# An MoE decoder layer on one core: narrower expert visits with two-sum matmuls, and expert rows added up per token in DRAM by GpSimd

## The reference, cut to what matters

```python
top_logit, top_e = lax.top_k(logits, TOP_K)          # 4 of 32 experts for a token
gates = jax.nn.softmax(top_logit, axis=-1)
xs = xf[tok]                                         # rows sorted by expert
hu = lax.ragged_dot(xs, w_gate_up, group_sizes) + b_gate_up[e_sorted]
gate = jnp.minimum(hu[:, :D_FF], SWIGLU_LIMIT)
up = jnp.clip(hu[:, D_FF:], -SWIGLU_LIMIT, SWIGLU_LIMIT)
act = (up + 1.0) * gate * jax.nn.sigmoid(SWIGLU_ALPHA * gate)
y = lax.ragged_dot(act, w_down, group_sizes) + b_down[e_sorted]
out = jnp.zeros_like(xf).at[tok].add(y * g_sorted[:, None])
h = layer_norm(ALPHA_RES * h + out, ln2_g, ln2_b)    # ALPHA_RES = 2 ** 0.25
```

## Time and profile before

| what | value |
|---|---|
| median of 3 runs | 4533.25 us |
| lowest, highest run | 4527.98, 4533.9 us |
| profiled execution, span from first to last instruction | 4529.3 us |
| PE busy | 4289.9 us, 95% of the span |
| DVE, ACT, POOL busy | 3076.1, 1817.6, 1010.1 us |
| DMA | 665.72 MB in all, mean 147 GB/s |

### The profile page before, as it was taken

The page is one execution under the profiler, slowest core; times in us unless marked ns, Lnnn a source line. Parts: engine busy times, 40 slices in busy tenths (PEclk is TensorE's granted clock), DMA queues, the critical chain, the costliest instruction groups (busy, mean ns, idle before and its releaser), DMA issues. The chain is left out here.

```text
span 4529.3 us, 70549 instructions
## 1 busy us (share of the span) xinstructions
PE 4289.9 (95%) x24356; PEld 3153.5 (70%) x24356; DVE 3076.1 (68%) x4861; ACT 1817.6 (40%) x2677; POOL 1010.1 (22%) x1152
## 2 busy tenths in 40 slices
PE   8999988999999998699999999999999999999987
PEld 4444434444444454599989889899999999999961
DVE  2587867878888873555556556666676777777768
ACT  1222223443434433233434444444445555555530
POOL 1111101221111122211112212222222222222235
PEclk9999989999999999799999999999999999999986
DMA  6443330120110010544555456474657667667668
GB/s 194 126 122 92 87 101 16 30 27 21 18 23 16 14 27 19 148 158 148 174 168 190 155 183 220 162 250 161 237 197 239 208 230 241 219 234 237 212 214 362
DMA packets 534140, 665.72 MB, mean 147 GB/s; under 512 B 64416, under 2 KB 402592, under 8 KB 533952
## 3 DMA queue, kind: packets, MB, share of 16 engines
q1 hardware_dynamic: 419664, 501.02, 34.7%
q10 hardware_dynamic: 87744, 77.15, 5.4%
q0 software_dynamic: 26576, 85.56, 5.0%
HBM read 543.61 MB, written 120.03 MB: 147 GB/s over the span
## 5 line engine op out<-in xcount | busy, mean ns | idle before, releaser
L2000 PE MATMUL gu<-x_hi,w_hi 128*128 128x240 f32 (+8 forms) x4096 | 1196.5, 292 | 4.1 <-issue 4.1
L2003 PE MATMUL gu<-x_lo,w_hi 128*128 128x240 f32 (+8 forms) x4096 | 1195.5, 292 | 0.5 <-issue 0.5
L2004 PE MATMUL gu<-x_hi,w_lo 128*128 128x240 f32 (+8 forms) x4096 | 1194.1, 292 | 0.0
L2106 DVE TENSOR_TENSOR w_lo<-w_raw,w_hi 128x2048 fp32r<-128x2048 f32 x386 | 874.6, 2287 | 414.1 <-ACT w_hi L2190 386.2
L2190 ACT ACTIVATE w_hi<-w_raw 128x2048 fp32r<-128x2048 f32 x386 | 726.8, 1908 | 207.4 <-PE gu L2004 132.0
L2000 PEld LDWEIGHTS gu<-x_hi,w_hi 128*128 128x128 f32 x4096 | 774.7, 189 | 4.5 <-issue 4.3
L2003 PEld LDWEIGHTS gu<-x_lo,w_hi 128*128 128x128 f32 x4096 | 773.3, 189 | 1.1 <-issue 0.9
L2004 PEld LDWEIGHTS gu<-x_hi,w_lo 128*128 128x128 f32 x4096 | 773.8, 189 | 0.0
L1972 POOL TENSOR_TENSOR a_lo<-up,a_hi 128x384 fp32r<-128x384 f32 x256 | 396.6, 1549 | 1177.8 <-ACT a_hi L2202 1177.8
L570 PE MATMUL proj_acc<-w_in_sb,hT 128*128 128x512 f32 (+1 forms) x1280 | 499.0, 537 | 0.7 <-ACT hT L586 0.7
L2000 PE MATMUL yp<-w_hi,a_hi 128*128 128x512 f32 x1088 | 445.6, 410 | 2.3
(11 more groups left out here) (316 smaller groups left out, 5878.6 us busy)
## 6 DMA issues: line engine op xcount, KB each, us to landing
w_raw<-w_gate_up SPq DMA_DIRECT2D x258, 1024.0 KB, 7.6
w_raw<-w_down SPq DMA_DIRECT2D x128, 1024.0 KB, 8.1
y_dram<-y_rows ACTq DMA_DIRECT2D x128, 256.0 KB, 2.6
y_dram<-zeros ACTq DMA_DIRECT2D x12, 2688.0 KB, 15.5
h_blk<-h_dram SPq DMA_DIRECT2D x32, 512.0 KB, 8.7
qi_dram<-qi_stage ACTq DMA_DIRECT2D x16, 640.0 KB, 3.2
x_in<-x SPq DMA_DIRECT2D x16, 512.0 KB, 6.1
w_in_sb<-w_in SPq DMA_DIRECT2D x4, 2048.0 KB, 14.2
```

Source lines behind the costliest of these rows:

```text
L2000: op = nc.tensor.matmul(out, s_hi_, m_hi, start=(n == 0), stop=False)
L2003: nc.tensor.matmul(out, s_hi_, m_lo, start=False, stop=False)
L2004: op = nc.tensor.matmul(out, s_lo_, m_hi, start=False, stop=(n == len(pairs) - 1))
L2106: nc.vector.tensor_tensor(w_lo[:, c % 2, cols], raw[:, c % 3, cols], w_hi[:, c % 2, cols].bitcast(F32), ALU.subtract).then_inc(s_lo, 1)
```

## The change

- Widths: `WIDTHS` becomes 384, 352, 320, 304, 288, 272, 256, 240, 208, 176. The counts then give 1, 3, 1, 4, 2, 6, 3, 5, 5 and 2 visits.
- For visits of at most 256 columns (15 of them), `two_sums` replaces `passes` in `up`: w_hi meets x_hi and x_lo in one matmul of 2 x width columns into two halves of a bank, and w_lo meets x_hi in a second one. DVE and ACT get a second body for these (`parted`): ACT copies the second half of both sums out of PSUM (`second_sums`), and DVE adds it to the first half. They work on 256 columns instead of 384.
- `y_dram` and the gathers of `combine_stage` go. `hold_places` and `hold_gates` on POOL make DRAM addresses and gates per row. ACT's `store` multiplies by the gate, and `scatter` on POOL adds each tile's rows into `sums` in DRAM with indirect DMAs (seven per visit). `sums` is first set to h1 in `attend_stage` (a second 512 KB store per block); `combine_stage` only loads it, adds the bias and normalizes, with one DVE pass less. The gates are scaled by 1 / ALPHA_RES.
- POOL's order in a visit: scatter 5 of the visit before; a_lo[0], a_lo[1]; `hold_places`; a_lo[2]; `hold_gates` and the list load of the next visit; a_lo[3]; gather 0; a_lo[4]; gather 1; a_lo[5]; gather 2; a_lo[6]; a_lo[7]; scatters 0 to 4.
- SP: `load_third` (three small value look-ups, a wait on `s_hold`, five small loads) stands before chunk 5 of each visit, and before the first chunk of all. The y stores go from SP and ACT.
- `lists` holds pairs (token, gate). The clearing of `y_dram` in `project_stage` goes (12 DMAs of 2.7 MB); `lists`, `h1` and `sums` get tail rows that are set in `attend_stage`.

```diff
-WIDTHS = tuple(range(ROWS, 2 * P - 17, -GRAIN))
+WIDTHS = (384, 352, 320, 304, 288, 272, 256, 240, 208, 176)
+KINDS = tuple((ROWS - width) // GRAIN for width in WIDTHS)
+LAST_KIND = tuple(kind - 1 for kind in KINDS[1:]) + KINDS[-1:]
+ONE_SUM = sum(width > 2 * P for width in WIDTHS)
...
+                for name in ("h1", "sums"):
+                    sp.dma_start(D_[name][SEQ:, :].rearrange("(m p) n -> p m n", p=P),
+                                 res[:].unsqueeze(1).broadcast_to([P, 1 + ROWS // P, D])).then_inc(s_clear, 16)
...
+                def load_third(v):
+                    at = look_up(sp, v, 1, MOST)
                     rest, few = (look_up(sp, v, what, 1) for what in (2, 3))
-                    rows, cols = [], []
+                    if not first(v):
+                        sp.wait_ge(s_hold, v)
                     for i in range(4):
...
+                        row = at + 2 * P + i * FEW - rest * ((i - i % 2) * FEW) - few * (i % 2 * FEW)
+                        sp.dma_start(third[i * FEW:(i + 1) * FEW], D_["lists"][bass.ds(row, FEW), :]
+                                     ).then_inc(s_third, 16)
...
+                    sp.dma_start(spot[:], A["spots"][bass.ds(rest + few, 1)].rearrange("o p j n -> (o p) j n")
+                                 ).then_inc(s_third, 16)
...
+                        if c == 5:
+                            load_third(v + 1)
...
+                def list_rows(v):
+                    at = look_up(pool, v, 1, MOST)
                     if not first(v):
                         pool.wait_ge(s_x, 48 * v)
                         pool.wait_ge(s_xt, 8 * v)
                     nc.gpsimd.dma_start(who[:], D_["lists"][bass.ds(at, ROWS), :].rearrange(
-                        "(m p) o -> p (m o)", p=P), allow_slow_non_contiguous=True).then_inc(s_who, 16)
-                    pool.wait_ge(s_who, 16 * v + 16)
-                    nc.gpsimd.tensor_tensor(who_now[:], who[:], zero[:], ALU.add)
+                        "(m p) o -> p m o", p=P), allow_slow_non_contiguous=True).then_inc(s_who, 16)
+                def gather(v, m):
+                    if m == 0:
+                        pool.wait_ge(s_who, 16 * v + 16)
+                        nc.gpsimd.tensor_tensor(who_now[:], who[:, :, 0], zero[:], ALU.add)
+                        pool.drain()
+                    nc.gpsimd.indirect_dma_start(
+                        x[:, m], None, D_["h1"], bass.IndirectOffsetOnAxis(ap=who_now[:, m:m + 1], axis=0)
+                    ).then_inc(s_x, 16)
+                def hold_places(v):
+                    if not first(v):
+                        pool.wait_ge(s_yst[0], 32 * v)
+                        pool.wait_ge(s_yst[1], 32 * v)
+                        pool.wait_ge(s_yst[2], 32 * v)
+                        pool.wait_ge(s_yst[3], 16 * v)
+                    pool.wait_ge(s_third, 80 * v + 80)
+                    nc.gpsimd.tensor_tensor(scaled[:], spot[:, :, 0], third[:, 0:1].broadcast_to([P, 3]), ALU.mult)
+                    for h in range(2):
+                        nc.gpsimd.tensor_scalar(at_main[:, :, h], who[:, 0:2, 0], 2.0, float(h), ALU.mult, ALU.add)
+                def hold_gates(v):
+                    nc.gpsimd.tensor_copy(gate_now[:, 0:2], who[:, 0:2, 1].bitcast(F32))
+                    nc.gpsimd.tensor_copy(gate_now[:, 2:3], third[:, 1:2].bitcast(F32))
                     pool.drain()
-                    for m in range(3):
-                        nc.gpsimd.indirect_dma_start(
-                            x[:, m], None, D_["h1"], bass.IndirectOffsetOnAxis(ap=who_now[:, m:m + 1], axis=0)
-                        ).then_inc(s_x, 16)
+                    nc.gpsimd.tensor_tensor(at_third[:], scaled[:], spot[:, :, 1], ALU.add).then_inc(s_hold, 1)
+                    pool.drain()
+                def scatter(v, n):
...
+                        parts = [(halves, at_main[:, n % 3, n // 3:n // 3 + 1], y[:, n % 3])]
+                    elif n == 2:
+                        parts = [(quarters, at_third[:, w:w + 1], y[:, 2, w * BANK // 2:(w + 1) * BANK // 2])
+                                 for w in range(2)]
+                    else:
+                        parts = [(halves, at_third[:, 2:3], y[:, 2])]
+                    for rows, at, part in parts:
+                        nc.gpsimd.indirect_dma_start(rows, bass.IndirectOffsetOnAxis(ap=at, axis=0), part, None,
...
+                        scatter(v - 1, 5)
                     for j in range(J):
+                        if j == 2:
+                            hold_places(v)
+                        elif j == 3:
+                            hold_gates(v)
+                            list_rows(v + 1)
+                        elif 4 <= j < 7:
+                            gather(v + 1, j - 4)
                         pool.wait_ge(s_ah, 8 * v + j + 1)
                         nc.gpsimd.tensor_tensor(a_lo[:, j], up[:, j % 2], a_hi[:, j].bitcast(F32), ALU.subtract)
                         nc.gpsimd.tensor_copy(a_rest[:, j], up[:, j % 2, 2 * P:2 * P + REST]).then_inc(s_al, 1)
+                    for n in range(5):
+                        scatter(v, n)
...
+                def two_sums(bank, width, triples):
+                    out = bank.rearrange("p (s n) -> p s n", s=2)[:, :, 0:width]
+                    for n, (w_high, w_rest, moving) in enumerate(triples):
+                        nc.tensor.matmul(out, w_high, moving, start=(n == 0), stop=False)
+                        op = nc.tensor.matmul(out[:, 0], w_rest, moving[:, 0], start=False, stop=(n == len(triples) - 1))
+                    return op
...
+                        g, u = g[:, 0:2 * P], u[:, 0:2 * P]
+                        dve.wait_ge(s_sig, 24 * v + 3 * j + 1)
+                        nc.vector.scalar_tensor_tensor(g, gu[:, j % 2, 0, 0:2 * P], b_gate, g, ALU.add, ALU.add)
+                        dve.drain()
+                        nc.vector.tensor_scalar(g, g, LIMIT, None, ALU.min).then_inc(s_gm, 1)
+                        dve.wait_ge(s_g1, 16 * v + 2 * j + 2)
+                        dve.wait_ge(s_sig, 24 * v + 3 * j + 2)
+                        nc.vector.scalar_tensor_tensor(u, gu[:, j % 2, 1, 0:2 * P], b_up, u, ALU.add, ALU.add
+                                                       ).then_inc(s_gu, 1)
+                        dve.drain()
+                        nc.vector.tensor_scalar(u, u, LIMIT, -LIMIT, ALU.min, ALU.max)
+                        dve.drain()
+                        nc.vector.scalar_tensor_tensor(u, u, 1.0, g, ALU.add, ALU.mult)
+                        return
...
+                def second_sums(v, j):
+                    act.wait_ge(s_g1, 16 * v + 2 * j + 1)
+                    nc.scalar.activation(gate[:, j % 2, 0:2 * P], gu[:, j % 2, 0, 2 * P:], ACT.Copy).then_inc(s_sig, 1)
+                    act.wait_ge(s_g1, 16 * v + 2 * j + 2)
+                    act.wait_ge(s_al, 8 * v + max(j - 1, 0))
+                    nc.scalar.activation(up[:, j % 2, 0:2 * P], gu[:, j % 2, 1, 2 * P:], ACT.Copy).then_inc(s_sig, 1)
...
+                    nc.vector.tensor_tensor(row, row, acc[:, slot], ALU.add).then_inc(s_tot, 1)
...
+                    nc.vector.scalar_tensor_tensor(row, row, small[:, slot, 12:13], gain[:], ALU.subtract, ALU.mult)
+                    dve.drain()
                     dve.wait_ge(s_rstd, t + 1)
-                    nc.vector.tensor_scalar(total[:, slot], total[:, slot], small[:, slot, 12:13], small[:, slot, 15:16],
-                                            ALU.subtract, ALU.mult)
-                    dve.drain()
-                    nc.vector.tensor_tensor(total[:, slot], total[:, slot], gain[:], ALU.mult)
-                    dve.drain()
-                    nc.vector.tensor_tensor(total[:, slot], total[:, slot], bias[:], ALU.add).then_inc(s_out, 1)
+                    nc.vector.scalar_tensor_tensor(row, row, small[:, slot, 15:16], bias[:], ALU.mult, ALU.add
...
```

More of the change, by code:

```diff
@@ L1977, in _ @@
                 pool.wait_ge(S["listed"], 64 * TILES)
-                gather(0)
+                list_rows(0)
+                for m in range(3):
+                    gather(0, m)
                 n = over_visits(pool, body)
+                scatter(n - 1, 5)
                 pool.wait_ge(s_x, 48 * n + 48)
-                nc.gpsimd.tensor_tensor(who_now[:], who[:], zero[:], ALU.add)
+                pool.wait_ge(s_yst[0], 32 * n)
+                pool.wait_ge(s_yst[1], 32 * n)
+                pool.wait_ge(s_yst[2], 32 * n)
+                pool.wait_ge(s_yst[3], 16 * n)
+                pool.wait_ge(s_third, 80 * n + 80)
+                nc.gpsimd.tensor_tensor(who_now[:], who[:, :, 0], zero[:], ALU.add)
             @block.tensor
@@ L2175, in _, with high @@
                     low_x(0, k)
-                over_visits(dve, body)
+                more = dve.value_load(S["more"][0:1, 0:1], min_val=EXPERTS - 1, max_val=MAX_VISITS - 1)
```

(10 more changed lines are left out.)

399 lines of the change are left out of this document (174 added, 225 removed).

## The result

The changed kernel takes 4565.99 us in the median (4563.06 to 4575.19) against 4533.57 (4527.98 to 4540.75) for the kernel before on the same chip: a ratio of 1.008, 95% interval 1.0068 to 1.0091, slower by 0.8%. The median is 32.4 us longer, where the prediction had 16.8 (4550 for 4533.25). The profiled execution has a span of 4566.2 us, 36.9 more than before's 4529.3.

The account below looks back on a forecast made before the run. Narrow visits were taken as bound by what PE streams, the end by gathers. Terms 6.8 + 9.5 + 18.5 + 14.7 - 34.9 + 1.4 + 1 = +17.0 gave span 4546.3, median 4550 us; range 4472 to 4610.

Parts of the forecast that it names:

- Widths: In `up`: two visits get wider (336 to 352, 368 to 384), 3.4 us each, +6.8 us.
- The gathers' new place: End of `up`: PE waits 8.7 + 0.3 + L - up/4 for gather 2, L issue to landing; +9.5 wide, +18.5 at 256 and 240.
- 208 and 176 columns bound by DVE: In `up`, DVE sets the pace, a_rest[5] at 40.2 us; with L 45.7 us against 43.59 in seven visits, +14.7.
- The term for the 12 visits of 240 columns and less: `up` plus the gather wait: +12.8 us for five visits of 240 and +14.7 for seven of 208 and 176.
- The no-wait rival, 4467: Last gather lands before `up` ends, so narrow visits keep 40 us saved; total -66, 4467 us; chance 0.18.
- The pair: In narrow `up`, two matmuls replace three: 8 ns saved per triple, 1.0 us a visit.
- it barely matters: Rival that the pair saves nothing in `up`: +8, 4558 us; only 3/4 counts where the gather ends last; no separate chance.
- Combine: After the experts: first sum 10.5 us earlier, fifteen steps at 5.48 us, experts' end 2.5 us later; -34.9 us.
- Slow adds: Scatter-adds take twice 7.5 us, so `store` 3 comes 4.2 us late; +48, 4598 us; chance 0.10.
- Start and attend: Before the first visit: `load_third(0)` and place stage +1.4 us, two small DVE operations a block in attend +1.

Follow-up runs that it names:

- chunk 5 out of the way: Changed kernel with the five small loads of `load_third` moved behind chunk 5's weight load on SP; 4569.14 us, ratio 1.0072 to the kernel before.
- The idle transposes: Changed kernel with 38, 54 or 60 unread identity transposes filling PE's gather wait at 240, 208, 176 columns; 4559.04 us, ratio 1.0037 to the kernel before.
- The best such kernel: Changed kernel with PE waiting for only two gathers up to 256 columns, gather 2 issued before a_lo[5], widths 208 and 176 removed; 4509.96 us, 0.9937.
- the two-tile wait: Changed kernel with gather 2 on its own semaphore, so visits up to 256 columns wait for two gathers: 4523.06 us, 0.9975; with gather 2 at j = 5: 0.9967.
- the later gather: Changed kernel with gather 2 issued one step later, at j = 7 behind a_lo[6]; 4709.47 us, ratio 1.037 to the kernel before.

## Why the prediction was right, and where not

The prediction said 4550 us, most likely slower, 4472 to 4610; 4566 lies 0.35% above it. The direction and the place of the loss were right, but the change cost nearly twice what was forecast. Step by step:

- **Widths**: right. The 352 and 384 visits that were narrower grew by 3.5 and 2.2 us, 5.7 for 6.8.
- **The gathers' new place**: right in its rule and its size. The prediction's 8.7 + 0.3 + L - up/4 gave 1.3 us at 272 columns, and the visits grew by 0.9 to 1.1; `up` plus wait was 46.15 at 240 and 45.7 below, and 46.6 and 46.4 came. L was 5.0 in the visits of 240 and less (taken: 5.2) and 4.2 in the wide ones (4.5). The 256 visits belonged with the wide ones, L 4.2, so their wait was 1.6 to 1.8 us and the sum 46.7 to 46.9, not 48.0. Its reason for 5.2, chunk 5 loading beside, is borne out: chunk 5 went at 29.5 us, and L is 4.2 with chunk 5 out of the way.
- **208 and 176 columns bound by DVE**: right for a_rest[5], at 41.1 us (40.2) at both widths; with L 0.2 shorter that is the +0.7 in each of seven visits. For `up` it is right in part. It ended at 40.2 us at 208 columns (39.4), but PE waited for DVE for 1.1 us of it; the rest is PE's own pace, for a pair took 0.300 us from start to start, 38.4 us for 128 of them, where the prediction had 37 in all. At 176 it ended at 39.3 and 40.9 (38.1), with pairs of 0.271 us, 34.7 in all for 32, and 3.7 us of waits for DVE. The 1.6 us between these two visits is clock again: behind the waits in the later one it was 0.79 over 8 us, in the earlier one 1.00. DVE itself was busy for 31.7 of 39.4 us there, not at all times.
- **The step that was mis-sized: a wait costs its own length.** The term for the 12 visits of 240 columns and less was 27.5 us; 57.3 came, and 22.6 of the difference is `down`, which took 27.05 us on average for 25.17. Behind these waits, all of 3.7 us and more, PE ran at 1.2 GHz for some microseconds. The prediction carried the clock into every window of the earlier trace rows and never asked what a new idle stretch in a stage of 1.00 would do to it, though the combine stage stood at 0.64 in the same rows. The idle transposes gave 20 us of it back in the eleven visits of the window. The other 7 us are the later a_rest[5] and the somewhat later end of the wait.
- **The no-wait rival, 4467**: its time was wrong, though not needed. It took PE as the next bound. With the wait gone the visits fell to 68.7 to 70.2 us, not 64.4, because a_rest[7] comes from DVE and POOL at 48.6 to 49.3 us at 240 columns and less. The best such kernel takes 4510 us, 0.9937 of the kernel before.
- **The pair**: its size was right, 0.328 us at 240 columns for three times 113.5 ns. In the changed kernel it is worth 2 to 4 us in all, behind two later bounds; "it barely matters" held.
- **Combine**: -34.1 for -34.9. The first sum starts 21.1 us behind the experts' last matmul, where the prediction's terms give 20.1; the fifteen steps take 81.5 us for 82.2, and what follows the last sum's start 11.6 for 11.0.
- **Slow adds**: did not come as time, though the adds are dear. Scatters landed in 3.7 to 8.9 us (medians of each scatter by its place in a visit), under the 10.8 us that the prediction worked out as the room of `store` 3; no wait of ACT for one is seen, and without the add the time is the same. The Trainium skill's statement that an add needs two source reads and halves the rate ("Collectives: The Full Stack", section "The bandwidth ceiling") points the right way: the scatters' share of the engines' time more than doubles, 12.8% with the add and 5.3% without, and the landing grows by less, 8.9 us for 6.6.
- **Start and attend**: -1.7 for +2.4, within the scatter of the first visit's start.

The chances leaned to slower for the right cause. The gain of the change sat in one place (combine) and was given back in another (the gathers behind a_rest[5]), and 22.6 of the some 65 us that the visits of 272 columns and less gave back was the clock. Without it the forecast would have been met within 3 us. That a sum without the clock still came so near in the total, 0.35%, is owed to the size of the rest of the kernel, not to the account.

## What to carry to other kernels

A wait of over 2 us put into this stream of matmuls mostly cost more than its length: price the slower matmuls behind it as well, and if the wait must stay, fill it. Ask of each wait whether what it waits for is read at all; here a semaphore of its own for the third gather was worth 1%. Before making the bounding engine faster, find the time at which its last operand is ready: an engine that arrives early at a fixed deadline only waits, and with the two-tile wait the narrower visits even came out slower (0.9967 for 0.9937). While the gather was late it was the other way round: without them the time was 0.4% longer. An edit is priced in the kernel in which it will stand.

## What was not expected of the hardware

- PE's pace fell to 0.427 us per 512 columns behind some waits and not behind others. Counted over the changed kernel and its twelve variants, at the end of `up` and in `down`: behind none of 54 waits of 1.0 to 1.9 us, behind 24 of 32 of 2.0 to 2.9 us (with 2.00 us `down` +1.5 us in one visit, no change with 2.65 in another), and behind all 91 of 3.0 us and more. What decides between 2.0 and 2.9 us is not shown. The slow stretch lasted 2.6 to 6.1 us and did not grow with the wait: in the visits of up to 240 columns `down` took 26.3 to 27.8 us in the changed kernel, behind 3.7 to 7.1 us, and 26.3 to 27.7 with the later gather, behind 6.4 to 9.9.
- Inside `up` too, waits for DVE of 1.7 to 2.7 us were followed by a lower clock in 15 of 34 cases.
- A VectorE clamp of 0.29 us took 1.93 us beside POOL's work, and a POOL product of 1.0 us took 2.5 beside a VectorE subtraction. Moving POOL's small steps by one unit cost DVE 24 us in 14 visits.
- The indirect add costs POOL 1.55 us an issue for 0.98 without the add, 2.2 us of landing in the one scatter that can be compared, and over twice the DMA engines' time, for nothing in the kernel's time.
- Taking two width classes away, which leaves the code of the other visits as it was, shortened `up` at 288 columns from 51.3 to 50.7 us and at 240 from 42.4 or 42.8 to 42.0, in both kernels in which it was done. But steps of this size come without an edit: the two 288 visits of the kernel before take 50.7 and 51.3 us. The cause is open.
